# Long and short matmuls in turn, and eight unread short ones behind two sums of squares, in a two-layer fp32 trunk

## What is computed

```
for layer in (0, 1):
    hn  = rms_norm(h, mix_norm[layer])
    h   = h + (attention(hn) if layer == 0 else rglru_block(hn))
    h   = h + square(relu(rms_norm(h, mlp_norm[layer]) @ w_up[layer])) @ w_down[layer]
return rms_norm(h, final_norm)
```

## Time and profile before

| | |
|---|---|
| median of three runs | 1996.98 us (1996.09 to 1997.16) |
| the profiled execution | 1997.17 us, of which the span is 1995.2 us |
| granted TensorE clock, mean | 0.999 of full |
| PE busy | 1981.6 us, 99% of the span |
| DVE, ACT busy | 1368.6 us, 1062.1 us |
| HBM read | 365.48 MB, 184 GB/s over the span |

### The profile page before, as it was taken

The page is one execution under the profiler, slowest core; times in us unless marked ns, Lnnn a source line. Parts: engine busy times, 40 slices in busy tenths (PEclk is TensorE's granted clock), DMA queues, the critical chain, the costliest instruction groups (busy, mean ns, idle before and its releaser), DMA issues.

```text
span 1995.2 us, 33969 instructions
## 1 busy us (share of the span) xinstructions
PE 1981.6 (99%) x11532; PEld 1735.6 (87%) x11532; DVE 1368.6 (69%) x1575; ACT 1062.1 (53%) x1446; POOL 7.3 (0%) x11
## 2 busy tenths in 40 slices
PE   9999999999999999999999999999999999999998
PEld 8898888888888888888888888888888888888887
DVE  7998676556656665666789997766566556656664
ACT  6666554444444444445588885544444444444453
POOL 1000000000000000000000000000000000000000
PEclk9999999999999999999999999999999999999999
DMA  8544565666555656556566655555665566555652
GB/s 286 158 127 153 175 200 185 195 187 191 188 187 177 198 188 189 178 179 200 190 190 189 189 169 188 191 190 189 191 188 184 195 180 198 186 188 177 199 175 95
DMA packets 365307, 368.17 MB, mean 185 GB/s; under 512 B 11472, under 2 KB 363856, under 8 KB 365136
## 3 DMA queue, kind: packets, MB, share of 16 engines
q1 hardware_dynamic: 364976, 365.53, 58.1%
q0 software_dynamic: 288, 2.10, 0.3%
HBM read 365.48 MB, written 2.10 MB: 184 GB/s over the span
## 4 chain that ended last, share of the span: by engine, by line
PE 94%; DVE 3%; ACT 2%; issue 1%; DMA 0%; DVEq 0%; SPq 0%; ACTq 0%
PE ps L1307 61%; PE ps L1310 30%; DVE w_lo L812 1%; ACT h L467 1%; PE aux L1327 1%; PE aux L1328 1%; PE aux L1329 1%; ACT w_hi L370 0%; DVE h L923 0%; DMA h<-x_l_dram 0%; DVE h L934 0%; PE aux L1382 0%; DVE u L826 0%; DVE pt L939 0%; DVE u L899 0%
## 5 line engine op out<-in xcount | busy, mean ns | idle before, releaser
L812 DVE TENSOR_TENSOR w_lo<-w_raw,w_hi 128x1024 fp32r<-128x1024 f32 x678 | 815.7, 1222 | 337.8 <-ACT w_hi L370 336.7
L370 ACT ACTIVATE w_hi<-w_raw 128x1024 fp32r<-128x1024 f32 x678 | 701.3, 1053 | 449.9 <-PE ps L1310 446.8
L1307 PE MATMUL ps<-xn,w_hi 128*128 128x512 f32 x2880 | 907.5, 396 | 2.5 <-DVE xn L880 2.3
L1307 PE MATMUL ps<-mid,w_hi 128*128 128x512 f32 x2544 | 799.4, 396 | 1.0 <-DVE w_lo L812 0.5
L1310 PEld LDWEIGHTS ps<-xn,w_lo 128*128 128x128 f32 x2880 | 541.7, 188 | 128.2
L1310 PEld LDWEIGHTS ps<-mid,w_lo 128*128 128x128 f32 x2544 | 477.9, 188 | 113.0
L1310 PE MATMUL ps<-xn,w_lo 128*128 128x256 f32 x2880 | 566.8, 278 | 0.0
L1310 PE MATMUL ps<-mid,w_lo 128*128 128x256 f32 x2544 | 500.1, 278 | 0.0
L1307 PEld LDWEIGHTS ps<-xn,w_hi 128*128 128x128 f32 x2880 | 439.6, 189 | 3.5 <-issue 2.9
L1307 PEld LDWEIGHTS ps<-mid,w_hi 128*128 128x128 f32 x2544 | 387.2, 189 | 1.8 <-DVE w_lo L812 0.9
L826 DVE TENSOR_TENSOR u<-ps,half 128x512 f32<-128x512 f32 x169 | 116.5, 690 | 155.3 <-ACT half L383 136.0
(11 more groups left out here) (168 smaller groups left out, 757.4 us busy)
## 6 DMA issues: line engine op xcount, KB each, us to landing
w_raw<-mlp_w_up_dram SPq DMA_DIRECT2D x256, 512.0 KB, 3.8
w_raw<-mlp_w_down_dram SPq DMA_DIRECT2D x256, 512.0 KB, 3.6
w_raw<-b_w_in_dram SPq DMA_DIRECT2D x64, 512.0 KB, 4.9
w_raw<-a_w_qkv_dram SPq DMA_DIRECT2D x40, 512.0 KB, 5.5
w_raw<-a_w_o_dram SPq DMA_DIRECT2D x32, 512.0 KB, 4.6
w_raw<-b_w_out_dram SPq DMA_DIRECT2D x32, 512.0 KB, 4.8
h<-x_l_dram SPq DMA_DIRECT2D x4, 512.0 KB, 8.6
gate_raw<-b_gate_a_w_dram SPq DMA_DIRECT2D x8, 256.0 KB, 2.8
```

Source lines behind the costliest of these rows:

```text
L370: nc.scalar.activation(w_hi[:, s, :, :], w_raw[:, slot, :, :], ACT.Copy).then_inc(hi_ready, 1)
L812: nc.vector.tensor_tensor(w_lo[:, s, :, :], w_raw[:, slot, :, :], w_hi[:, s, :, :].bitcast(F32), ALU.subtract).then_inc(lo_ready, 1)
L1307: nc.tensor.matmul(ps[:, 2 * half_i + b, :], hi[:, k, b * PART:(b + 1) * PART], operand[:, :, kt, :], start=kt == 0, stop=False)
```

## The change

`products` gets a parameter `in_turn`. Without it the order is as before: long b0, long b1, short b0, short b1 for each k. With it, b is the outer loop and k the inner one, and each long matmul is followed by its short one: eight matmuls into the bank of b = 0, long and short in turn, then eight into that of b = 1. It is used in the second pair of each mixer's first quad and in all its other quads, in recurrent quads 1 to 7, and in chunks 0, 1 and 2 of the attention pairs that have `g_before`. The other calls keep their order: the first quad, the first attention pair, chunk 3 of the others, both output projections, the first recurrent quad, and the first pair of each mixer.

In both mixers, `stats` is followed by eight matmuls of 256 columns that write the scratch area `x0` of a bank of `aux`; nothing reads what they write.

```diff
+RUN = 8
...
-            def products(q, half_i, s, operand, ready_sem, ready, late=False):
+            def products(q, half_i, s, operand, ready_sem, ready, late=False, in_turn=False):
...
-                for k in range(CH_KT):
+
+                def long(k, b):
                     kt = s * CH_KT + k
+                    nc.tensor.matmul(ps[:, 2 * half_i + b, :], hi[:, k, b * PART:(b + 1) * PART],
+                                     operand[:, :, kt, :], start=kt == 0, stop=False)
+
+                def short(k, b):
+                    kt = s * CH_KT + k
+                    return nc.tensor.matmul(ps[:, 2 * half_i + b, TOK:2 * TOK], lo[:, k, b * PART:(b + 1) * PART],
+                                            operand[:, 0, kt, :], start=False, stop=kt == KT - 1)
+
+                if in_turn:
                     for b in range(2):
...
+                        for k in range(CH_KT):
+                            long(k, b)
+                            last = short(k, b)
+                else:
+                    for k in range(CH_KT):
+                        long(k, 0)
+                        long(k, 1)
+                        short(k, 0)
+                        last = short(k, 1)
                 last.then_inc(wts_used, 1)
...
-                pair(q, half_i, *qkv, between)
+                pair(q, half_i, *qkv, between, (0, 1, 2) if g_before is not None else ())
...
+            def stats_and_run(n):
+
+                stats(n)
+                for _ in range(RUN):
+                    nc.tensor.matmul(x0[:, 0:TOK], xn[:, 0, 0, 0:PART], xn[:, 0, 0, :], start=True, stop=True)
+
             def mlp(base, norm, mid_base):
                 operand = (xn, xn_ready, 8 * norm)
-                quad(base, *operand, {3: lambda: stats(norm)})
+                whole = tuple(range(CHUNKS))
+                quad(base, *operand, {3: lambda: stats_and_run(norm)}, (), whole)
                 with pe.Fori(1, 4) as i:
-                    quad(i + base, *operand)
+                    quad(i + base, *operand, None, whole)
...
-                quad(n + QB_IN, *lru_in, {0: lambda: gates(n - 1)})
+                quad(n + QB_IN, *lru_in, {0: lambda: gates(n - 1)}, tuple(range(CHUNKS)))
```

More of the change, by code:

```diff
@@ L1303, in products @@
                 hi, lo = late_w if late else (w_hi[:, s], w_lo[:, s])
-                for k in range(CH_KT):
+                def long(k, b):
                     kt = s * CH_KT + k
-                    for b in range(2):
[L1307 to L1311, removed]
+                    nc.tensor.matmul(ps[:, 2 * half_i + b, :], hi[:, k, b * PART:(b + 1) * PART],
+                                     operand[:, :, kt, :], start=kt == 0, stop=False)
@@ L1312, in products, with pair, quad @@
                 last.then_inc(wts_used, 1)
-            def pair(q, half_i, operand, ready_sem, ready, between=None):
+            def pair(q, half_i, operand, ready_sem, ready, between=None, in_turn=()):
                 for s in range(CHUNKS):
-                    products(q, half_i, s, operand, ready_sem, ready)
+                    products(q, half_i, s, operand, ready_sem, ready, in_turn=s in in_turn)
                     if between and s in between:
                         between[s]()
-            def quad(q, operand, ready_sem, ready, between=None, between_b=None):
-                pair(q, 0, operand, ready_sem, ready, between)
-                pair(q, 1, operand, ready_sem, ready, between_b)
+            def quad(q, operand, ready_sem, ready, between=None, in_turn=(), in_turn_b=None):
+                pair(q, 0, operand, ready_sem, ready, between, in_turn)
+                pair(q, 1, operand, ready_sem, ready, None, in_turn if in_turn_b is None else in_turn_b)
@@ L1443, in _ @@
                 quad(i + QB_WO, *att)
+            def stats_and_run(n):
+                stats(n)
+                for _ in range(RUN):
+                    nc.tensor.matmul(x0[:, 0:TOK], xn[:, 0, 0, 0:PART], xn[:, 0, 0, :], start=True, stop=True)
             def mlp(base, norm, mid_base):
                 operand = (xn, xn_ready, 8 * norm)
-                quad(base, *operand, {3: lambda: stats(norm)})
+                whole = tuple(range(CHUNKS))
+                quad(base, *operand, {3: lambda: stats_and_run(norm)}, (), whole)
                 with pe.Fori(1, 4) as i:
-                    quad(i + base, *operand)
+                    quad(i + base, *operand, None, whole)
                 with pe.Fori(0, 4) as i:
-                    quad(i + (base + 4), mid, mid_ready, mid_base)
+                    quad(i + (base + 4), mid, mid_ready, mid_base, None, whole)
                 with pe.Fori(1, GROUPS) as g:
                     with pe.Fori(0, 4) as i:
-                        quad(g * 8 + i + base, *operand)
+                        quad(g * 8 + i + base, *operand, None, whole)
                     with pe.Fori(0, 4) as i:
-                        quad(g * 8 + i + (base + 4), mid, mid_ready, g * PAIRS + mid_base)
+                        quad(g * 8 + i + (base + 4), mid, mid_ready, g * PAIRS + mid_base, None, whole)
             mlp(QB_MLP0, 1, MID_MLP0)
```

## The result

The changed kernel takes 2018.58 us (median of four runs, 2017.34 to 2019.96) against 1997.07 for the kernel before: ratio 1.0108, 95% interval 1.0096 to 1.0121. The profiled execution's span is 2016.6 us against 1995.2, 21.4 more. The runs of the changed kernel lie within 2.7 us of each other, and 1998.51 is the highest of the kernel before. Lines have moved: the long product is line 1308 now, the short one 1313, the sums 1349 and 1350, the eight unread shorts 1464.

The account below looks back on a forecast made before the run. PE was taken as the bound, by matmul count and step. On the profiled 1997.17 us, -7.8 for 578 calls and +1.9 for the unread shorts gave 1991.3, or 1991.1 us from the median; 8-in-10 range 1974 to 2001.

Parts of the forecast that it names:

- What bounds the kernel: Whole kernel: PE, busy 99%, bounds it; time is the number of matmuls by the start-to-start step.
- What an alternating pair costs: All 578 changed calls: 0.3467 us a pair against 0.3483, as on gate tiles; 7.8 us less.
- the calls come in two kinds of stretches: Sign in the profile after that the forecast was wrong: rhythm lost in places, only part of 578 calls gains.
- the pair sum rose above 674: Sign of a wrong forecast: means of long and short sum above 674 ns; about 671 was expected.
- high end 0.353: Upper bound for an alternating pair: a long as slow as today's (0.233 us) and a short of 0.120.
- alternation is the slower rhythm: Rival for all 578 calls: shorts 0.120, longs 0.233, 37 ns more a call, 2020 us; chance 0.16.
- which tile the weights come from, or what was running before: Gate-tile calls against others: suggested outside causes for a matmul's cost beyond its columns, a few ns per k.
- weight loads that hide under longs: Changed calls: each short's weight load has a whole long (0.233 us) to hide under, a reason for the better rhythm.
- The eight unread shorts: Behind the sums in both mixers: sixteen matmuls at 0.1196 us add 1.9 us, bounds 1.8 to 2.3.
- What they can do ... I price that at nothing: Unread shorts may leave PE in the rhythm of a run of shorts, as gates and scores do; priced at nothing.
- Attention and recurrent calls: 74 calls gain 13.5 ns each, 1.0 us in all, not eaten by DVE.
- The rule of the Trainium skill: Columns at 2.4 GHz plus about 2.5 ns: 325 ns a pair in either order, reorder gains nothing; reaching it, some 1891 us.

Follow-up runs that it names:

- Experiment 7: Kernel before with a 32-byte pad ahead of the high weight tiles, moving every tile behind `w_raw`; 2012.39 us.
- experiments 4: Changed kernel, with the eight unread shorts taking their weights from the gate tile instead of from the operand; 1991.76 us.
- 6: Changed kernel, with the weights of the eight unread shorts 8 floats (32 bytes) further on in the operand; 1991.76 us.
- experiment 12: Changed kernel, second pair of each mixer's first quad in old order, eight unread shorts moved between its first four quads and the fifth; 2015.78 us.
- 13: Changed kernel without unread shorts; second pair of each mixer's first quad in old order, turn begun after the first k of its last call; 2016.87 us.
- 14: As 13, also in turn: last three quads of both output projections, first pair of both mixers and of the recurrence; 1988.52 us, ratio 0.9957 to the kernel before.
- experiment 1: Changed kernel without the eight unread shorts (RUN = 0); 2015.57 us.
- experiment 2: Changed kernel with 24 unread shorts in place of eight (RUN = 24); 2023.01 us.
- experiment 8: Changed kernel with a 32-byte pad ahead of the high weight tiles; 2022.13 us.

## Why the prediction was wrong, point by point

**What bounds the kernel** was right: PE alone, by the number of matmuls and the step between them. PE has no new wait, DVE stayed hidden in attention and the recurrent quads, and calls times the cost of a call, with the eight shorts, give 21.1 of the 21.4 us that the span grew.

**The step that failed** is "What an alternating pair costs", where I took one value, 0.3467, for all 578 calls. It gave 1991.1 us with a range of 1974 to 2001; the measured 2018.58 lies above it, in the part to which I had given a chance of 0.16. For the 74 calls of attention and recurrence it is right: seven pairs in 2.43 us. In the 504 of the mixers a pair takes 0.3533. Two of the signs that I had named came true: the calls come in two kinds of stretches, and the pair sum rose above 674, to 679. My bounds contained the pair (high end 0.353), and the rival "alternation is the slower rhythm" gave 2020 against 2018.58, but that it came so close is luck. It made all 578 calls slow, and its reason was not what happened: shorts did not go to 0.120 with longs at 0.233. In the three pairs of the timeline the longs take 0.71 us together (0.237 each) and the shorts 0.35 (0.117), and the same order is fast elsewhere.

**What I missed is that the rhythm is a state.** I had seen in the earlier trace rows that identical shapes can go at 0.693 or 0.697 a k, and had put it down to "which tile the weights come from, or what was running before". I then took the better value of two short calls as that of long stretches, and argued for it from weight loads that hide under longs. The same order with the same loads goes at 0.3467 and at 0.3533, so that argument cannot decide between them. Experiment 7 shows that the place does set the steps of such a call and still does not give the better rate over a long stretch; experiments 4, 6, 12 and the pair 13 and 14 show that in the mixers it is what ran before that decides. A cost that depends on history can't be carried from one place in a kernel to another by its shapes.

**The eight unread shorts** cost what was forecast: 8 take 1.14 us from 272.90 to 274.04, of which some 0.18 is the restart behind the sums that the first long paid before. "What they can do ... I price that at nothing" was the costly sentence: in the changed kernel they lead into the slow rhythm (as do the bare sums, experiment 1), and 32 bytes further on they lead into the fast one, worth 26.8 us. I had likened them to the gates' run; the size is the same and the count made no difference (experiment 2), but the place of the weights isn't the same.

**Attention and recurrent calls**: fast in the trace, and too few to see in the time (1996.53 against 1996.28).

**The rule of the Trainium skill** ("TensorE: Matmul & The Clock Gate", section "Back-to-back issue gap") gives an estimated 325 ns for a pair in any order, by a formula that it states for an isolated matmul. Here pairs took 346.7, 348.3, 351 and 353.3 ns by the order, the place and what came before; no run came near 325.

What stays open is the mechanism. The runs show what switches the rhythm (a run's weights 32 bytes further on, one k more or less of the old order) while the calls themselves stay the same. Other distances than 32 bytes were not tried. Why the steps of PE's matmuls lock into one pattern or the other, and why seven shorts of eight at the good place are not enough, no run here tells.

## What to carry to other kernels

When PE is full and all waits are gone, count matmuls per stretch to four digits and compare equal calls in different stages: if they differ at the same clock, PE may be in different rhythms, and what stands ahead of the stage can matter as much as what is in it. After any reordering near the start of a long stage, measure that count again, since a harmless edit of a few matmuls can move hundreds of calls by 2%. And a rate read at one place in a trace is only evidence for another if the work ahead of both is the same.

## What the runs showed that I had not expected

- A long and a short product of fp32r (512 and 256 columns) in turn have two steady rates, 0.3467 and 0.3533 us a pair, at the same granted clock of 1.00, on the same tiles. Each lasted to the end of its stage (up to 252 calls, 0.7 ms).
- Eight unread matmuls in the middle of a fast stage made the rest of it slow (experiment 12: 2015.78 against 1989.01).
- The weights of those eight, 32 bytes further on in the same tile, gave the other rhythm (1991.76 against 2018.58).
- All weight tiles, and the tiles behind them, 32 bytes further on made the old order slower, 0.351 us for 0.348 (2012.39 against 1997.1).
- The old order has two phases of equal rate, k by k (0.47 + 0.23 and 0.46 + 0.24), and which of them stands ahead of the turn went with the rate behind it in all ten mixer entries tried (1989 against 2017 us, 1988.5 against 2015.3).
- With the pad, the recurrent quads went from the fast rate to the slow one (0.3533 us a pair, experiment 8), behind a run of gates whose weights had moved by 32 bytes.
